# Two feed-forward stages on TensorE: output blocks computed in pairs, matmuls in turn into two PSUM banks, with two pairs of banks

## What is computed

```
D_MODEL = 1024; SEQ = 512; D_FF = 4 * D_MODEL

def squared_relu_mlp(n, w_up, w_down):
    return jnp.square(jax.nn.relu(n @ w_up)) @ w_down

# at the end of each of the two layers
h = h + squared_relu_mlp(rmsnorm_2(h, g_ffn[layer]), w_up[layer], w_down[layer])
```

## Time and profile before

| | us |
|---|---|
| median of 3 runs | 1756.25 |
| lowest and highest of them | 1753.19, 1757.21 |
| profiled execution: span from first to last instruction | 1751.1 |
| of it PE busy | 1670.4 |
| `ffn0`, from its first matmul | 349.1 |
| `stick` and `outc` between the two stages | 255.8 |
| `ffn1`, from its first matmul | 349.3 |

### The profile page before, as it was taken

How to read it: one execution, slowest core, us unless ns; L and a number is a source line. 1 busy time by engine, 2 the same in 40 slices (tenths; PEclk the granted TensorE clock), 3 DMA queues, 4 the chain that set the end, 5 groups by cost and what they waited for, 6 DMA issues and landing times.

```text
span 1751.1 us, 20132 instructions
## 1 busy us (share of the span) xinstructions
PE 1670.4 (95%) x7650; PEld 1343.6 (77%) x7650; DVE 901.2 (51%) x1157; ACT 604.1 (34%) x799; POOL 266.1 (15%) x213
## 2 busy tenths in 40 slices
PE   6999999999999688999999999999998999999999
PEld 5877777778776567768888888888776788888887
DVE  6424444474767787545343434447765453434343
ACT  5323222314244144343222222347665432222121
POOL 3001211103232224322010101200000220101010
PEclk9999999999989899999999999999999999999999
DMA  4222222222211111122222222222120222222222
GB/s 173 100 93 72 72 72 72 96 96 77 92 49 48 48 64 48 49 72 97 96 97 97 96 97 95 97 96 73 49 73 24 97 96 97 97 96 96 96 97 96
DMA packets 24723, 146.56 MB, mean 84 GB/s; under 512 B 3648, under 2 KB 4944, under 8 KB 7760
## 3 DMA queue, kind: packets, MB, share of 16 engines
q1 hardware_dynamic: 24656, 145.62, 23.7%
HBM read 143.52 MB, written 2.10 MB: 83 GB/s over the span
## 4 chain that ended last, share of the span: by engine, by line
PE 83%; DVE 11%; ACT 2%; issue 2%; POOL 1%; DMA 0%; DVEq 0%; ACTq 0%; SPq 0%; POOLq 0%
PE ps_G L392 25%; PE ps_G L393 25%; PE ps_G L394 25%; PE ps_AV L497 2%; PE ps_C L468 2%; DVE wide L1692 1%; PE ps_C L487 1%; DVE top L1688 1%; PE ps_ST L455 1%; ACT Sb L951 1%; DVE cl L1443 1%; POOL Sb L1281 1%; DVE tmp L1414 1%; PE ps_SX L619 0%; DVE tmp L1415 0%
## 5 line engine op out<-in xcount | busy, mean ns | idle before, releaser
L392 PE MATMUL ps_G<-nh,wh 128*128 128x512 f32 x1056 | 415.3, 393 | 8.0 <-DVE nl L1844 5.5
L393 PE MATMUL ps_G<-nl,wh 128*128 128x512 f32 x1056 | 412.0, 390 | 0.0
L394 PE MATMUL ps_G<-nh,wl 128*128 128x512 f32 x1056 | 411.8, 390 | 0.0
L901 ACT ACTIVATE wh<-raw 128x2048 fp32r<-128x2048 f32 x131 | 250.0, 1908 | 319.0 <-PE ps_G L394 304.6
L392 PE MATMUL ps_G<-ch,wh 128*128 128x512 f32 x880 | 354.8, 403 | 2.1 <-DVE fb L1584 2.1
L393 PE MATMUL ps_G<-cl,wh 128*128 128x512 f32 x880 | 344.9, 392 | 0.0
L394 PE MATMUL ps_G<-ch,wl 128*128 128x512 f32 x880 | 344.7, 392 | 0.0
L1389 DVE TENSOR_TENSOR wl<-raw,wh 128x2048 fp32r<-128x2048 f32 x119 | 274.3, 2305 | 134.3 <-ACT wh L901 130.9
L392 PEld LDWEIGHTS ps_G<-nh,wh 128*128 128x128 f32 x1056 | 198.9, 188 | 58.0 <-issue 10.7
L394 PEld LDWEIGHTS ps_G<-nh,wl 128*128 128x128 f32 x1056 | 198.8, 188 | 41.7
L393 PEld LDWEIGHTS ps_G<-nl,wh 128*128 128x128 f32 x1056 | 198.9, 188 | 40.5 <-issue 0.2
(11 more groups left out here) (212 smaller groups left out, 1627.4 us busy)
## 6 DMA issues: line engine op xcount, KB each, us to landing
raw<-wst SPq DMA_DIRECT2D x132, 1024.0 KB, 4.8
h<-xT SPq DMA_DIRECT2D x8, 256.0 KB, 5.6
outT<-h SPq DMA_DIRECT2D x8, 256.0 KB, 2.0
tabs<-rb_d SPq DMA_DIRECT2D x1, 1024.0 KB, 10.9
tabs<-tab_d SPq DMA_DIRECT2D x1, 1024.0 KB, 4.9
tabs<-tab_d SPq DMA_DIRECT2D x1, 512.0 KB, 4.1
small<-small_d SPq DMA_DIRECT2D x1, 192.0 KB, 8.2
small<-swap_d SPq DMA_DIRECT2D x1, 128.0 KB, 4.0
```

What stands on the lines that cost most here:

```text
L392: mm(o, ah, bh, start=first, stop=False)
L393: mm(o, ah, bl, start=False, stop=False)
L394: return mm(o, al, bh, start=False, stop=last)
L901: A(wh[s][:], raw[s][:], ACT.Copy).then_inc(w_hi, 1)
```

## The change

It touches only `ffn0` and `ffn1`. Two blocks of a tile are computed together by `project_pair`: for each chunk six matmuls, in turn into two banks. The pairs of blocks take two pairs of banks in turn, named F0/F1 and F2/F3, which are C0/C1 and G0/G1 under semaphores of their own. Because of that PE waits before each stage until C0, C1, G0 and G1 have been read out, and after `ffn0` until the last four blocks have been; ACT waits for the last block too. The wait of ACT before splitting a tile is now for the second block of the pair two tiles ago. DVE's, ACT's and POOL's orders stay as they are, on the new banks.

```diff
@@ STAGES
-          ("ffn0", 4, 8, 16), ("stick", 4, 3, 6), ("outc", 2, 2, 4), ("ffn1", 4, 8, 16)]
+          ("ffn0", 4, 8, 0), ("stick", 4, 3, 6), ("outc", 2, 2, 4), ("ffn1", 4, 8, 0)]
...
+class Pairs(Step):
+    def __init__(self, name, i):
+        super().__init__(name, i)
+        self.part, self.base = i, 16 if name == "ffn1" else 0
+    def bank(self, k):
+        return f"F{2 * (k // 2 % 2) + k % 2}"
+    def block_use(self, k):
+        return self.part * 4 + (k // 4 + self.base)
+    def freed(self, kb):
+        n = kb // 2 - 1
+        return f"F{2 * (n % 2) + 1}", self.part * 4 + (n // 2 + 1 + self.base)
...
+        ps |= {"F0": ps["C0"], "F1": ps["C1"], "F2": ps["G0"], "F3": ps["G1"]}
...
+            def project_pair(st, k, tile, xh, xl, each=None):
+                o = [take_block(st, k + a) for a in range(2)]
+                s = st.slot(tile)
+                for c in range(KC):
+                    if each is not None:
+                        each(c)
+                    first, last = c == 0, c == KC - 1
+                    hi = [wh[s][:, c, a * P:(a + 1) * P] for a in range(2)]
+                    lo = [wl[s][:, c, a * P:(a + 1) * P] for a in range(2)]
+                    for a in range(2):
+                        mm(o[a][:], hi[a], xh[:, c, :], start=first, stop=False)
+                    for a in range(2):
+                        mm(o[a][:], hi[a], xl[:, c, :], start=False, stop=False)
+                    for a in range(2):
+                        ins = mm(o[a][:], lo[a], xh[:, c, :], start=False, stop=last)
+                        if last:
+                            give_block(ins, st, k + a)
...
@@ PE, mlp
-                    st = Step(name, i)
-                    for k in range(8):
-                        if k % 2 == 0:
-                            need_tile(st, k // 2)
-                        project(st, k, k // 2, k % 2 * P, mh, ml, each=fed_by(n) if first and k == 0 else None)
+                    st = Pairs(name, i)
+                    for k in range(0, 8, 2):
+                        need_tile(st, k // 2)
+                        project_pair(st, k, k // 2, mh, ml, each=fed_by(n) if first and k == 0 else None)
...
-                    for k in range(8, 16):
-                        if k % 2 == 0:
-                            need_tile(st, k // 2)
-                        project(st, k, k // 2, k % 2 * P, oh, ol, each=hidden if k == 8 else None)
+                    for k in range(8, 16, 2):
+                        need_tile(st, k // 2)
+                        project_pair(st, k, k // 2, oh, ol, each=hidden if k == 8 else None)
+
+                for b in range(2):
+                    passed(pe, moved[f"C{b}"], count[f"C{b}"] if name == "ffn1" else use[("score", 12, b)][1])
+                for k in (2, 3):
+                    stands(pe, Step("outc" if name == "ffn1" else "outab", 1), k)
                 part(0, first=True)
...
             mlp("ffn0", 3, 0)
             pe.wait_ge(masks_set, 1)
+            for k in range(12, 16):
+                stands(pe, Pairs("ffn0", 3), k)
...
@@ ACT, split
-                passed(act, done["G1"], st.block_use(kb))
+                b, n = st.freed(kb)
+                passed(act, done[b], n)
...
@@ ACT
             mlp("ffn0", 0, ("norm", 3), 4)
+            passed(act, done["F3"], 16)
```

More of the change, by code:

```diff
@@ L274, in stands @@
         def stands(eng, st, k):
-            passed(eng, moved[f"G{st.bank(k)}"], st.block_use(k) + 1)
+            passed(eng, moved[st.bank(k)], st.block_use(k) + 1)
         def ready(eng, key):
@@ L362, in _ @@
             for k in range(KC):
-                stands(sp, Step("ffn1", 3), 8 + k)
+                stands(sp, Pairs("ffn1", 3), 8 + k)
                 sp.dma_start(out[k * P:(k + 1) * P, :], h[:, k, :]).then_inc(stored, 16)
@@ L380, in take_block @@
             def take_block(st, k):
-                passed(pe, moved[f"G{st.bank(k)}"], st.block_use(k))
-                return ps[f"G{st.bank(k)}"]
+                passed(pe, moved[st.bank(k)], st.block_use(k))
+                return ps[st.bank(k)]
             def give_block(ins, st, k):
-                ins.then_inc(done[f"G{st.bank(k)}"], 1)
+                ins.then_inc(done[st.bank(k)], 1)
             def need_tile(st, k):
@@ L406, in project @@
                 give_block(last, st, k)
+            def project_pair(st, k, tile, xh, xl, each=None):
[15 more added lines that the diff above has]
+                            give_block(ins, st, k + a)
             def project_some(st, k, xh, xl, chunks, first, last):
-                o = take_block(st, k) if first else ps[f"G{st.bank(k)}"]
+                o = take_block(st, k) if first else ps[st.bank(k)]
                 s, col = st.slot(k // 2), k % 2 * P
@@ L997, in _ @@
                                  scale=rt[:, t:t + 1])
-                    last.then_inc(moved[f"G{st.bank(k)}"], 1)
+                    last.then_inc(moved[st.bank(k)], 1)
                 else:
@@ L1010, in _ @@
                     tanh_half(wide[:, bass.ds(i * 4 + k, 1), :].rearrange("p a n -> p (a n)"), st, k).then_inc(
-                        moved[f"G{st.bank(k)}"], 1)
+                        moved[st.bank(k)], 1)
             with act.Fori(0, 4) as i:
@@ L1391, in ready_block @@
             def ready_block(st, k):
-                passed(dve, done[f"G{st.bank(k)}"], st.block_use(k) + 1)
-                return ps[f"G{st.bank(k)}"][:]
+                passed(dve, done[st.bank(k)], st.block_use(k) + 1)
+                return ps[st.bank(k)][:]
             def moved_block(ins, st, k):
-                ins.then_inc(moved[f"G{st.bank(k)}"], 1)
+                ins.then_inc(moved[st.bank(k)], 1)
                 stands(dve, st, k)
@@ L1584, in _ @@
                         stt(out=fb[:, 0, :], in0=at(wide, 8), scalar=1.0, in1=ready_block(st, k),
-                            op0=ALU.add, op1=ALU.mult).then_inc(moved[f"G{st.bank(k)}"], 1)
+                            op0=ALU.add, op1=ALU.mult).then_inc(moved[st.bank(k)], 1)
                         moved_block(stt(out=fb[:, 1, :], in0=at(wide, 0), scalar=1.0, in1=ready_block(st, k + 1),
```

14 lines of the change are left out of this document (8 added, 6 removed).

## The result

The changed kernel takes 1764.87 us (median of 4 runs, 1762.89 to 1768.99), the one before 1754.72 (4 runs, 1751.17 to 1757.21). The ratio is 1.0068 with a 95% interval of 1.0047 to 1.0089: slower by 8 to 16 us. A second set on another occasion, further down, gave 1.0047 (1.0029 to 1.0064).

The account below looks back on a forecast made before the run. The prediction took PE's stream of 226.7 ns matmuls as the bound; 2.2 + 1.0 + 3.1 + 1.7 + 0.5 = 8.5 us on the 1751.1 us span gave 1759.6, plus 5.2 to the median 1764.8 us, range 1758 to 1770.

Parts of the forecast that it names:

- What bounds the kernel: Both feed-forward stages: PE never waits, so only the fixed 13.3 ns of each matmul could be won, 40.9 us at most.
- Part 1: Matmuls of `ffn0` and `ffn1`: alternating banks gain 0 us; -40.9 us if all of the fixed part goes.
- The estimate of 33 us: Both stages: the skill page's 216 ns step against 226.7 would leave some 10.9 ns a matmul, over 3072 matmuls, to win.
- the oscillation: Both stages, rival: PE idles between turns and its clock falls in a tenth of 698 us, 35 us more; chance 0.04.
- Part 2: Start of `ffn0` and `ffn1`: PE waits 1.1 us each for the projection's last block, +2.2 us, bounds 2.0 and 2.4.
- Part 3: Blocks finish in twos: PE waits 0.5 us for the tile after pair 1 in both stages, +1.0 us, bounds 0 and 2.3.
- the other covers: Later up pairs, up-to-down turn, down pairs and SP's loads: work hidden behind PE stays hidden, costed at nothing.
- Part 4: End of `ffn0`: `stick` waits for the last pair's blocks, +3.1 us, and half clock after it, +1.7 us (0 to 3.4).
- Part 5: End of the kernel: block 15's add starts later, right behind block 14's, +0.5 us, up to 1.2.
- The sum: Whole kernel: all terms together add 8.5 us to the profiled span of 1751.1; 5.6 with all low, 12.4 all high.
- The bank as fixed cost: Rival, both stages: changing banks removes all 13.3 ns a matmul, 1724 us, or half of it, 1744; chance 0.10.
- vanishing waits: Rival, `stick`: its idle PE time takes back the 3 us lost before it, total 1758 to 1760 us; chance 0.06.

Follow-up runs that it names:

- experiment 6: Kernel before, with `ffn1` up blocks multiplying constant bfloat16 tiles and down blocks using one constant float32r weight tile; one run, 1753.43 us.
- Experiment 3: Changed kernel, but in the last part of `ffn0` DVE adds both blocks of a pair before making the two low parts; 1759.97 us, ratio 1.0039.
- experiment 1: Changed kernel with the second pair of banks on C2 and AV in place of G0 and G1; 1756.43 us, ratio 1.0009 to the kernel before.

## Why the prediction was right

*What bounds the kernel.* Right. In the kernel before both stages ran without a hole, and the step of 226.7 ns was the only thing to win.

*Part 1, the turns, 0 us.* Right, and this carried the forecast. 3072 matmuls that change bank each time take what 3072 did that changed every 24th time. The boundary step in the earlier trace rows was a fair sample. What the fixed part is I left open; experiment 6 takes 10.6 of its 13.3 ns away with bfloat16 from constant tiles. The estimate of 33 us drawn from the Trainium skill ("TensorE: Matmul & The Clock Gate", "Back-to-back issue gap") was right as a step of bfloat16, 216 ns in experiment 6, and not to be had in this kernel's type. The granted clock stayed at 1.00 in both stages, so the oscillation that the Trainium skill describes in the same page's "A second HAM failure mode: psum-queue depth-cycling" did not come.

*Part 2, the starts, 2.2 us.* Measured 2.8, outside my bounds of 2.0 to 2.4. The term left out was the way from DVE's add back into PE: 0.31 us, where I had taken under 0.1 from a hand-over from DVE to ACT, and 0.08 for the steps after a stop. The price of a hand-over has to be read on the engine that receives it. The size of this term was wrong, its place and its reason were not.

*Part 3, 1.0 us, nothing elsewhere.* Measured 0.9, at the place named, for the reason named; the other covers held.

*Part 4, 3.1 and 1.7 us.* Measured 3.3 and 0.08 for the stop, and 1.7. Experiment 3 shows the chain. The hand-over into PE was too small here as well, 0.47 us where I had 0.1. For the clock I took the longer of two gaps as the rule, and that does not hold: a gap of 2.5 us kept the clock in the kernel before and lost it in the changed one (gap from 1340.9, half clock from 1344.1). That the 1.7 us came in both profiles is in part luck.

*Part 5, 0.5 us.* Measured 0.4.

*The sum, 8.5 us.* 8.9 in the changed places of the profile; 10.2 between the medians, and 8.2 us by the ratio of the second set. That the median met the forecast to 0.1 us is luck. I had added 5.2 us, the distance from the profiled span to the median of the three runs, as if it carried over. But every run on record with its own span is only 1.7 to 2.1 us above it, so about 3 of the 5.2 us were a profiled execution that happened to be a fast one; for the changed kernel the distance is 0.8. What made this good are the 4.1 us ahead of `ffn0`, which have nothing to do with the change. The kernel before, too, has a median 1.5 us lower with its fourth run.

*The rivals.* The bank as fixed cost is refuted by the steps, vanishing waits by the gap of 3.56 us, which with the half clock behind it passed on in full until late in `stick`: `stick` and `outc` grew by 4.7 us.

## What to carry to other kernels

A stream of matmuls whose starts are evenly spaced and never wait can be sped up only by a shorter step; look in the trace for the places where the suspected cause is already absent (here: the steps across a bank change) before rebuilding the order around it. If blocks are finished in twos, the second is read out late, and PE stands where the next stage wants its bank: giving the pairs banks that neither neighbour uses (experiment 1) took away most of what the change cost, but whatever is made from the late block is late all the same. When PE does stop, count 0.3 to 0.5 us from the reader's last write to the next matmul, and after a stop like the 3.6 us one here 1.7 us for the half clock behind it.

## What the runs showed of the hardware that I had not expected

- A float32r matmul of 512 columns steps by 226.7 ns with its own 128 weight columns from changing places, by 230 ns with 64 weight columns, and by 233 ns when each loads the same tile. bfloat16 with neighbouring elements, from constant tiles, steps by 216 ns. Why less or repeated weight makes float32r slower was not found out.
- Mixed with float32r, dense bfloat16 loses its advantage (2 ns in three matmuls), and bfloat16 read at every second element makes three matmuls 23 ns longer.
- In the first 480 us the clock fell for 3.4 us not at all, once or twice behind the same 1.5 us gaps, in code common to all kernels: 1.6 us later each time in the changed kernel's first profile. Late in `stick` gaps of 2.5 to 2.8 us lost the clock in some profiles and kept it in others; the one of 4.6 us lost it in all ten. Two profiles of kernels that differ little can be 4 us apart by that before they reach the changed code.
